# Experts that skip padded rows, 512-wide gate and up with the down product a block behind, and a half-column inversion

## What is computed

```python
sol = lax.linalg.triangular_solve(a_mat, rhs, left_side=True, lower=True, unit_diagonal=True)   # per head and chunk

# 64 experts, top 8 of each token; assignments sorted by expert into blocks of 128 rows,
# each block of one expert, padded with rows of weight zero (token t: none)
row_tok = jnp.full((n_rows,), t, jnp.int32).at[dest].set(tok_s)
row_w = jnp.zeros((n_rows,), xf.dtype).at[dest].set(w_s.astype(xf.dtype))
hid = jax.nn.silu(xblk @ w_gate[e]) * (xblk @ w_up[e])          # 1024 -> 256, twice
yb = hid @ w_down[e]                                            # 256 -> 1024
y = jax.ops.segment_sum(yb * row_w[:, None], row_tok, num_segments=t + 1)
```

## Time and profile before

| | us |
|---|---|
| median of 3 runs | 3029.82 (3026.61 to 3031.46) |
| profiled execution, time | 3023.12 |
| profiled execution, span | 3021.5 |
| PE busy | 2568.9 (85%) |
| DVE busy | 1833.5 (61%) |
| ACT busy | 1327.4 (44%) |
| POOL busy | 770.9 (26%) |
| granted PE clock, mean | 0.937 |

### The profile page before, as it was taken

The page is one execution under the profiler, slowest core; times in us unless marked ns, Lnnn a source line. Parts: engine busy times, 40 slices in busy tenths (PEclk is TensorE's granted clock), DMA queues, the critical chain, the costliest instruction groups (busy, mean ns, idle before and its releaser), DMA issues. The chain is left out here.

```text
span 3021.5 us, 44783 instructions
## 1 busy us (share of the span) xinstructions
PE 2568.9 (85%) x14616; PEld 2148.4 (71%) x14617; DVE 1833.5 (61%) x2585; ACT 1327.4 (44%) x1859; POOL 770.9 (26%) x901
## 2 busy tenths in 40 slices
PE   6989998998999899969969841899999898998891
PEld 5768777877777777847857631787887777887781
DVE  3346887788688755536536521566656677556745
ACT  3343453355345333334322100566656666555741
POOL 2002211222221111100002062343433333333333
PEclk8989999999999999989979875899999999999996
DMA  5523335432333353253543236999999999899974
GB/s 99 73 39 67 64 50 53 68 50 44 70 71 46 67 70 85 64 198 112 167 164 118 67 42 146 276 276 296 278 272 270 289 306 334 241 270 271 336 173 148
DMA packets 346842, 462.88 MB, mean 153 GB/s; under 512 B 22569, under 2 KB 278057, under 8 KB 346735
## 3 DMA queue, kind: packets, MB, share of 16 engines
q1 hardware_dynamic: 311966, 343.37, 43.8%
q0 software_dynamic: 34768, 118.05, 15.4%
HBM read 367.21 MB, written 94.10 MB: 153 GB/s over the span
## 5 line engine op out<-in xcount | busy, mean ns | idle before, releaser
L57 PE MATMUL gu_ps<-e_hi,xg_hi 128*128 128x256 f32 x1488 | 435.9, 293 | 30.3 <-DVE e_lo L2274 16.5
L57 PE MATMUL dn_pj<-x_hi,dn_hi 128*128 128x512 f32 x1024 | 438.9, 429 | 11.1 <-DVE dn_lo L910 9.0
L59 PE MATMUL gu_ps<-e_hi,xg_lo 128*128 128x256 f32 x1488 | 422.6, 284 | 0.0
L58 PE MATMUL gu_ps<-e_lo,xg_hi 128*128 128x256 f32 x1488 | 422.0, 284 | 0.0
L59 PE MATMUL dn_pj<-x_hi,dn_lo 128*128 128x512 f32 x1024 | 410.5, 401 | 0.0
L58 PE MATMUL dn_pj<-x_lo,dn_hi 128*128 128x512 f32 x1024 | 409.6, 400 | 0.0
L994 DVE SCALAR_TENSOR_TENSOR uc_half<-u_in,par,uc_half 128x512 f32<-128x512 f32 x480 | 383.4, 799 | 13.1
L2215 ACT ACTIVATE e_hi<-e_raw 128x1024 fp32r<-128x1024 f32 x256 | 265.7, 1056 | 169.2 <-DMA e_raw<-in_w_up_e_dram 168.8
L57 PEld LDWEIGHTS gu_ps<-e_hi,xg_hi 128*128 128x128 f32 x1488 | 288.4, 194 | 58.9 <-DVE e_lo L2274 31.4
L2274 DVE TENSOR_TENSOR e_lo<-e_raw,e_hi 128x1024 fp32r<-128x1024 f32 x256 | 303.0, 1219 | 37.8 <-ACT e_hi L2215 37.2
L58 PEld LDWEIGHTS gu_ps<-e_lo,xg_hi 128*128 128x128 f32 x1488 | 286.1, 192 | 1.3
(11 more groups left out here) (348 smaller groups left out, 5226.0 us busy)
## 6 DMA issues: line engine op xcount, KB each, us to landing
e_raw<-in_w_gate_e_dram SPq DMA_DIRECT2D x256, 256.0 KB, 6.4
e_raw<-in_w_up_e_dram SPq DMA_DIRECT2D x256, 256.0 KB, 6.9
e_raw<-in_w_down_e_dram SPq DMA_DIRECT2D x128, 512.0 KB, 9.3
dn_raw<-in_w_in_dram SPq DMA_DIRECT2D x64, 512.0 KB
gate_rows<-qkv_next SPq DMA_DIRECT2D x16, 512.0 KB, 2.9
br_raw<-in_w_oa_dram SPq DMA_DIRECT2D x16, 512.0 KB
br_gate<-gate_rows SPq DMA_DIRECT2D x32, 256.0 KB, 4.2
br_raw<-in_w_ob_dram SPq DMA_DIRECT2D x16, 512.0 KB
```

The costliest lines, as they stand in the source:

```text
L57: nc.tensor.matmul(out, w_hi, x_hi, start=first, stop=False)
L58: nc.tensor.matmul(out, w_hi, x_lo, start=False, stop=False)
L59: return nc.tensor.matmul(out, w_lo, x_hi, start=False, stop=last)
```

## The change

In the experts:

- A padded row carries the number 32768, and gather and adding store have `bounds_check=S - 1, oob_is_err=False`, so that rows outside the table are skipped. The spare rows and the zeros that `mix_norm` wrote into them are gone.
- The gather lands in a new buffer `x_landing`; POOL copies it to `x_gather` (`hand_over`) when PE has transposed the block before. The row numbers of the stores wait in a table `late_rows`; a store is of the block four back (`LAG`).
- Gate|up is one product 512 wide. The down product of a block stands behind the gate|up product of the next. The row's weight is applied by DVE with the hidden.
- A gate/up piece is four k of one matrix, one DMA of 512 KB with runs of 4 KB.
- ACT and DVE do the first four weight pieces at the start of a block, the last two at its end. The first three experts are written out, the others in a loop; SP loops over single experts.

In the delta net each level multiplies only the left half of each diagonal block (`left`): 64 moving columns instead of 128, `y_sb` and the subtraction half as large. The last level works on one 64x64 quarter of each matrix.

```diff
-                link(g.memset(junk[:], 0.0))
-                g.iota(junk[:, :, 0:1].rearrange("p (n c) o -> p n (c o)", c=P), pattern=[[0, HALF // P], [1, P]],
-                       base=S, channel_multiplier=0, allow_small_or_imprecise_dtypes=True).then_inc(fill_ready, 2)
+                link(g.memset(junk[:], NONE))
+                g.memset(junk[:, :, 1:2], 0.0).then_inc(fill_ready, 2)
...
+            def left(x, l, u=None):
+
+                b = 1 << l
+                v = x[:].rearrange("p u (m r) -> p u m r", r=2 * b)
+                return v[:, :, :, 0:b] if u is None else v[:, u, :, 0:b]
...
-                            last = mm(ga[:, u, :], atl[l % NA][:, u, :], xx[:, u, :], start=True, stop=True)
+                            last = mm(ga[:, u, 0:P // 2], atl[l % NA][:, u, :], left(xx, l, u), start=True, stop=True)
...
-                                last = mm(gb[:, u, :], xt[:, u, :], yy[:, u, :], start=True, stop=True)
+                                last = mm(gb[:, u, 0:P // 2], xt[:, u, :], yy[:, u, :], start=True, stop=True)
                             else:
-                                last = mm(gb[:, u, :], yy[:, u, :], xt[:, u, :], start=True, stop=True)
+                                last = mm(gb[0:P // 2, u, 0:P // 2], yy[:, u, :], xt[:, u, P // 2:P], start=True, stop=True)
...
-                        A(yy[:].rearrange(FLAT), ga[:].rearrange(FLAT), ACT.Copy).then_inc(y_evac, 1)
+                        A(yy[:], ga[:, :, 0:P // 2], ACT.Copy).then_inc(y_evac, 1)
...
-                        tt(dst[:], dst[:], gb[:], ALU.subtract).then_inc(x_upd, 1)
+                        if l < LEVELS - 1:
+                            dst, z = left(xx, l), dense(gb[:, :, 0:P // 2], l)
+                        else:
+                            dst, z = xt[0:P // 2, :, P // 2:P], gb[0:P // 2, :, 0:P // 2]
+                        tt(dst, dst, z, ALU.subtract).then_inc(x_upd, 1)
...
-                pool.dma_start(self.x1_d[S:NROW, :], zero[:]).then_inc(z_out, 16)
-                pool.dma_start(self.y_d[S:NROW, :], zero[:]).then_inc(z_out, 16)
...
+                if i < 4:
+                    ks, w = slice(4 * (i // 2), 4 * (i // 2) + 4), i % 2
+                    return raw[i][:].rearrange("p (k f) -> p k f", k=4), wh[j][:, ks, w, :], wl[j][:, ks, w, :]
+                return raw[i][:], dh[j][:, i - 4, :], dl[j][:, i - 4, :]
...
+                def gather(n, column):
+
                     alone(pool, self.passed)
+                    g.tensor_copy(idx_g[:], self.tok_tab[:, column]).then_inc(idx_c, 1)
+                    g.tensor_copy(late_rows[:, bass.ds(n + LAG, 1)], self.tok_tab[:, column]).then_inc(idx_l, 1)
+                    pool.wait_ge(idx_c, n + 1)
+                    alone(pool, self.passed)
+                    pool.indirect_dma_start(xl_d[:], None, self.x1_d, bass.IndirectOffsetOnAxis(idx_g[:, 0:1], 0),
+                                            bounds_check=S - 1, oob_is_err=False).then_inc(xg_in, 16)
+
+                def hand_over(n):
+
+                    pool.wait_ge(xg_in, n * 16 + 16)
+                    pool.wait_ge(t_done, n * 2 + 2)
+                    alone(pool, self.passed)
+                    g.tensor_copy(xg[:], xl_d[:]).then_inc(x_here, 1)
+                    pool.wait_ge(x_here, n + 1)
+
+                def scatter(n):
+
+                    pool.wait_ge(scat, n * 16 + 16)
+                    pool.wait_ge(idx_l, n + 1)
+                    alone(pool, self.passed)
+                    g.tensor_copy(idx_s[:], late_rows[:, bass.ds(n, 1)]).then_inc(idx_t, 1)
+                    pool.wait_ge(idx_t, n + 1)
+                    pool.wait_ge(y_ready, n + 1)
                     alone(pool, self.passed)
                     pool.indirect_dma_start(self.y_d, bass.IndirectOffsetOnAxis(idx_s[:, 0:1], 0), yb[:], None,
-                                            compute_op=ALU.add).then_inc(scat, 16)
+                                            bounds_check=S - 1, oob_is_err=False, compute_op=ALU.add).then_inc(scat, 16)
...
+                g.memset(xl_d[:], 0.0).then_inc(init, 1)
+                g.memset(yb[:], 0.0).then_inc(y_ready, LAG)
+                g.memset(late_rows[:, 0:LAG], int(NONE)).then_inc(init, 1)
+                pool.sem_inc(t_done, 2)
+                pool.dma_start(self.credit_d[0], self.ong[:]).then_inc(scat, 16)
...
+                        gather(n, bass.ds(e * NT + b, 1))
+                        scatter(n)
+                        hand_over(n)
...
+                for late in range(LAG):
+                    scatter(total + late)
...
+                def blk(e, j, j_prev, gb, first):
+
+                    pe.wait_ge(xl_s, gb * 2 + 1)
                     if first:
+                        pe.wait_ge(lo_s, e * PIECES + 2)
+                    gate_up(j, range(0, 4))
+                    pe.wait_ge(xl_s, gb * 2 + 2)
+                    if first:
+                        pe.wait_ge(lo_s, e * PIECES + 4)
+                    gate_up(j, range(4, 6))
+                    transposes(gb + 1)
+                    gate_up(j, range(6, 8)).then_inc(gu_done, 1)
+                    if j_prev is not None:
+                        down(j_prev, gb - 1)
+                    hid_t(gb)
...
+                def y_move(gb):
                     act.wait_ge(y_done, gb + 1)
+                    act.wait_ge(scat, (gb + LAG) * 16 + 16)
+                    A(yb[:], fl(yp[:]), ACT.Copy).then_inc(y_ready, 1)
+
+                def blk(gb, prev, split):
+
+                    split(0, 1, 2, 3)
+                    act.wait_ge(gu_done, gb + 1)
+                    A(sg[:], gu[:, 0, :], ACT.Silu).then_inc(sg_s, 1)
+                    for b in range(2):
+                        act.wait_ge(t_done, gb * 2 + 5 + b)
+                        x_hi(b)
+                    if prev:
+                        y_move(gb - 1)
+                    act.wait_ge(ht_done, gb + 1)
+                    A(hh[:], ht[:], ACT.Copy).then_inc(hh_s, 1)
                     split(4, 5)
...
+                def blk(e, b, gb, split):
+                    split(0, 1, 2, 3)
+                    dve.wait_ge(sg_s, gb + 1)
+                    v.scalar_tensor_tensor(out=hid[:], in0=sg[:], scalar=self.wt_tab[:, bass.ds(e * NT + b, 1)],
+                                           in1=gu[:, 1, :], op0=ALU.mult, op1=ALU.mult).then_inc(hid_s, 1)
                     x_lo(gb + 1, 0)
                     x_lo(gb + 1, 1)
+                    dve.wait_ge(hh_s, gb + 1)
+                    tt(hl[:], ht[:], hh[:].bitcast(F32), ALU.subtract).then_inc(hl_s, 1)
+                    split(4, 5)
```

272 lines of the change are left out of this document (88 added, 184 removed).

## The result

| | before | after |
|---|---|---|
| median, us | 3030.51 (3026.61 to 3031.46, 4 runs) | 2996.44 (2989.52 to 2998.54, 4 runs) |
| ratio | | 0.9884, 95% interval 0.9865 to 0.9903 |
| span of the profiled execution | 3021.5 | 2994.6 |

The change made the kernel 34 us faster. The prediction said 75 us faster (2955), so its direction and its stated range hold, and its size is off by more than half. The time is that of rival (a), 3000; whether its mechanism is there is another matter.

The account below looks back on a forecast made before the run. In the experts TensorE and the DMA engines were both taken as near their end. The terms -80 - 15 + 25 - 8 + 3 = -75 us gave 2948 from the profiled execution, 2955 us as median; range 2885 to 3030.

Parts of the forecast that it names:

- rival (a): Experts: Pool's loop keeps today's pace, 11.3 us a block, time 3000; chance 0.20, shared with skipped rows costing like real ones.
- TensorE in a block: Experts: a block without waits falls from 10.46 to 9.6 us on TensorE, 80 us less over 93 blocks.
- DMA engines: Experts: 4 KB runs save 90 us and skipped rows 103 us of DMA time, 997 to about 804 us; landings shorten.
- The term of 15 us: Experts: what shorter DMA landings take off the 99 us that are no TensorE work.
- The Pool loop: Experts: a round with the new copy takes 10.9 us at today's landings, 9.5 if they fall to 5.5.
- ACT and VectorE: Experts: some 9.5 us of work each per block, before and after; counted as 0, inside the 25 us added for loops.
- lump of 25: Experts: 0.3 us a block, 25 us in all, added for three loops of about 10 us that wait for each other.
- Conversions ahead of the silu: Experts: ACT's four early conversions might let a late load delay silu and x_hi; counted 0, named as sign of error.
- Rival (b): Experts: Pool's x copy and VectorE's conversions take turns, a 12.7 us round, 110 us more, time 3132; chance 0.12.
- Delta net: Inversion: half the columns save ACT and VectorE work, no gain on TensorE passes; 8 us less, between 0 and 34.
- case (e): Delta net: a pass of 64 columns costs half of 0.11 us, 79 us below the forecast, 2876; chance 0.02.
- The ends: Start and end of the kernel: another memset, a credit DMA wait and four late stores; +3 us, from -5 to +10.

Follow-up runs that it names:

- e1_delta_only: The kernel before with nothing but the half-column inversion of the delta net; 0.9952 of the kernel before.
- e9_direct_lag3: The changed kernel without Pool's copy: gather straight into x_gather, store three blocks back, row numbers ahead of the transposes' wait; 0.9936 of the kernel before.
- e10_direct3_order: e9_direct_lag3 with the third and fourth weight piece converted behind x on ACT and VectorE; 0.9666 of the kernel before, 2918.4 us.
- e14_half_store: The changed kernel with the adding store also skipping the rows of tokens 512 and above; 0.9822 of the kernel before.

## Why the prediction was half right

- **TensorE in a block**: right. The block without waits is 9.33 us (forecast 9.6), 9.7 to 9.8 in the blocks that pause for 0.4 us behind the hidden's transposes, and by the ledger own work fell by 72 us, where 80 were forecast. 512-wide products start 0.23 apart, as said.
- **DMA engines**: the mechanism is right, the size isn't. The share is 0.82 (forecast 0.78), the DMA time 857 us for 997 (forecast 804), and the rate at full share 252 / 0.82 = 307 GB/s. The landings fell as forecast: over all of the stretch the gather's median is 5.5 us (6.9 before, forecast 5 to 6) and the store's 7.7 (9.4 before, forecast 7.5). But they spread: one store in ten still takes 10.3 us or more (10.0 before), and an engine that waits sees the late ones. The term of 15 us is mis-sized: taken away one by one, the two parts cost 15 to 20 and 25 to 30 us.
- **The Pool loop**: the copy was taken at 1.1 us; it is 1.04 alone and 1.29 in the mean, up to 2.1. A round fits TensorE's block, as the forecast says, and TensorE doesn't wait for it. The register loads of a new expert, taken at 0.9, are 2.1 in Pool's timeline. I held Pool's round against TensorE's block, and so missed its other customer: the store stands in the same list, and what the copy and loads add delays its issue.
- **ACT and VectorE: 0, inside a lump of 25, and no term for the clock**: this is the step that failed. "The scatter loop stays [...] ACT, which is in order, waits in y_move" was seen, and its price put into the lump. Waits and clock together were to be 10 us more (25 less the 15 of relief); they are 49 more, 19 of waits and 30 of clock. TensorE's waits for VectorE are 90 us instead of 67, by way of what stands behind y_move on ACT (the hidden's high part, six conversions) and behind those on VectorE. More than their sum their length changed: the longest wait for the hidden is 6.9 us instead of 2.7, and of TensorE's waits 36 are over 1.5 us instead of 10. The forecast let the clock go on at 0.99, as if longer pauses had no price of their own; it is 0.95. That the two engines have 9.5 us of work each is true; the sum of busy times says nothing of a chain that crosses from one to the other four times in a block.
- **Conversions ahead of the silu**: named as what would make the prediction wrong ("a new wait of ACT at the first four conversions that PE sees as waiting for the hidden"). TensorE does wait for the hidden; ACT's wait is not for the weights (19 us in all), it is for the store.
- **Rival (a)** has the time (3000) without the mechanism: TensorE waits for Pool's copy once. **Rival (b)**'s mechanism exists. Pool's copy and VectorE's conversions take turns: four low parts are 4.63 us alone, mostly 5.5 and up to 5.99 with Pool's copy beside, 0.15 us each in the mean. The Trainium skill (SBUF — State Buffer, section SBUF: two separate sides) has VectorE and GpSimd share a lock on one port pair; the trace agrees, 1220 ns without the copy, 1374 with it. Its price isn't (b)'s 110 us: 38 of the 93 copies take over 1.2 us, 45 of the 256 low parts over 1.3, and Pool's round has room.
- **Delta net**: forecast 8, measured 7.0 to 7.7 in the two profiles. Passes of 64 columns are (1.00 - 0.27) / 7 = 0.104 us apart, 0.11 before, so case (e) is out, and so is the estimate of 43 us worked from the Trainium skill (TensorE: Matmul & The Clock Gate, section Back-to-back issue gap) without the weight load.
- **The ends**: +3 forecast, +8 measured at the end (four late stores, one behind the other). The start gave 8.6 that nobody counted: TensorE's first wait for a weight's low part is 2.0 us instead of 9.0 (ahead of the delta net), since ACT can round the weights issued at 55.4 us at 68.2, where it was 56.7 and 76.7; e1_delta_only has it at 8.2. Which of the changed DMAs or memsets did that wasn't tried.

Luck has a part in it: the relief is worth 40 to 50 us, if its two parts add up, and not 15. Had it been the 15, the time would stand between 3021 and 3031, at the edge of the stated range.

What stays open: what the second buffer would be worth without its branches; what starts the waits for x's low part (34 us), which are short only in e9_direct_lag3 and e10_direct3_order (12 and 4 us); how much of e14_half_store's gain is the store's landing and how much the traffic; and why x lands 0.8 us earlier when VectorE's conversions are spread.

## What to carry to other kernels

List for each in-order engine what stands behind each wait, and price a late DMA by everything behind it, through to the engine that sets the pace; busy sums per engine don't see it. Before adding work to a queue engine, look at all that the queue issues: here a copy for the gather delayed the store, and the store's landing held ACT. When a wait moves and TensorE's waits stay (129, 242, 63 and 199 us on ACT in four orders, 102 to 112 us on TensorE), look for the buffer behind it: here dropping the copy and spreading the conversions together made 0.9666 of the kernel before, where the change alone is 0.9884. Price long pauses twice, once as waits and once by the clock behind them. And read a DMA's landing from all of its kind: those that somebody waited for are the late ones.

## What the runs showed of the hardware

- Pool and VectorE hold each other up: a 128x1024 copy on Pool is 1.04 us, up to 2.13 beside conversions; a copy of 128x1 is 0.18 or 1.2; a conversion on VectorE is 1.22 us, and 1.37 to 1.42 in the mean with one or two copies a block.
- The issue of a gather on Pool takes 1.07 us, and 1.89 beside a conversion on VectorE.
- An adding store whose out-of-bounds rows are skipped lands sooner: 6.4 us in the median with half of its rows left out, 7.6 with all real ones, 9.0 with the padded rows stored too.
- After pauses of 3 and 2 us TensorE ran 13 products at a granted clock of 0.50: 2.6 us more on a pause of 5. Over the experts the kernel with 110 us of waits lost 36 us that way, the one with 91 us in shorter pieces 6.
- Two branches by a register's parity ahead of Pool's store cost 1.1 us a round.
